# First gated rows two chunks later, the exponentials of two stages two chunks earlier, and the first gate load issued first

## The reference

```
scores = einsum('thpd,pnd->thpn', q, sub_keys)        # 8 heads, 2 x 128 keys
sv, si = top_k(scores, 16)
cand   = sv[:, :, 0, :, None] + sv[:, :, 1, None, :]
cv, ci = top_k(cand, 16)                              # 16 of 256 pairs per head
e_idx  = si0[ci // 16] * 128 + si1[ci % 16]
gates  = softmax(cv)
a      = einsum('thkd,td->thk', u_tab[e_idx], x)
wgt    = gelu(a) * gates
out    = einsum('thk,thkd->td', wgt, v_tab[e_idx])
```

## Time and profile before

| | |
|---|---|
| median of three executions | 1734.02 us |
| the profiled execution | 1737.73 us, its span 1735.8 us |
| TensorE busy | 1623.5 us, 94% of the span |
| VectorE busy | 1319.8 us, 76% |
| ScalarE busy | 689.5 us, 40% |
| GpSimd busy | 653.5 us, 38% |
| mean granted TensorE clock | 0.978 |
| chain that ended last | PE 70%, DVE 22%, DMA 4% |
| 8 stores of gates, issue to landing | 9.1 us shortest, 11.5 median, 28.3 longest |

### The profile page before, as it was taken

The page is one execution under the profiler, slowest core; times in us unless marked ns, Lnnn a source line. Parts: engine busy times, 40 slices in busy tenths (PEclk is TensorE's granted clock), DMA queues, the critical chain, the costliest instruction groups (busy, mean ns, idle before and its releaser), DMA issues.

```text
span 1735.8 us, 23134 instructions
## 1 busy us (share of the span) xinstructions
PE 1623.5 (94%) x8238; PEld 1376.8 (79%) x8238; DVE 1319.8 (76%) x2726; ACT 689.5 (40%) x1036; POOL 653.5 (38%) x450
## 2 busy tenths in 40 slices
PE   3999999986999999899986999999989999999996
PEld 3787776775899999899986898988966667766775
DVE  7489776987588899789934988988975555555589
ACT  4335565424333454545542343343323333333332
POOL 2010000002127788657652745746624423232311
PEclk9999999997999999999998999999999999999998
DMA  7423235453666567667767989889779999999962
GB/s 279 159 83 113 95 96 177 143 180 123 243 245 199 149 167 182 170 182 196 201 215 267 361 319 363 347 310 371 271 264 366 402 362 355 357 369 374 346 249 79
DMA packets 181682, 422.29 MB, mean 243 GB/s; under 512 B 33600, under 2 KB 66496, under 8 KB 181568
## 3 DMA queue, kind: packets, MB, share of 16 engines
q1 hardware_dynamic: 91472, 264.44, 42.5%
q0 software_dynamic: 57200, 139.58, 23.8%
q10 hardware_dynamic: 32896, 16.78, 3.5%
HBM read 375.55 MB, written 45.15 MB: 242 GB/s over the span
## 4 chain that ended last, share of the span: by engine, by line
PE 70%; DVE 22%; DMA 4%; ACT 2%; issue 2%; SPq 0%; DVEq 0%; ACTq 0%
PE bank L1676 21%; PE bank L1677 20%; PE bank L1678 20%; PE bank L1955 3%; DVE one L1468 2%; DVE one L1466 2%; DVE wlo L1300 2%; DVE one L1470 2%; DMA gates_by_key<-stage 2%; DVE raw L990 1%; DMA vraw<-in_v_tab_dram 1%; PE bank L1769 1%; PE bank L1754 1%; PE bank L1904 1%; DVE stats L1001 1%
## 5 line engine op out<-in xcount | busy, mean ns | idle before, releaser
L1676 PE MATMUL bank<-act_hi,whi 128*128 128x384 f32 (+1 forms) x1352 | 483.6, 358 | 22.4 <-ACT gelz L869 15.5
L1677 PE MATMUL bank<-act_lo,whi 128*128 128x384 f32 (+1 forms) x1352 | 473.9, 351 | 0.0
L1678 PE MATMUL bank<-act_hi,wlo 128*128 128x384 f32 (+1 forms) x1352 | 473.8, 350 | 0.0
L1676 PE MATMUL bank<-vhi,eh 128*128 128x512 f32 x768 | 305.4, 398 | 10.2 <-DVE vlo L1508 10.2
L1677 PE MATMUL bank<-vlo,eh 128*128 128x512 f32 x768 | 301.8, 393 | 0.0
L1678 PE MATMUL bank<-vhi,el 128*128 128x512 f32 x768 | 300.9, 392 | 0.0
L1676 PEld LDWEIGHTS bank<-act_hi,whi 128*128 128x128 f32 x1352 | 257.1, 190 | 40.5 <-issue 20.9
L1508 DVE TENSOR_TENSOR vlo<-vraw,vhi 128x512 fp32r<-128x512 f32 x256 | 176.6, 698 | 127.1 <-ACT vhi L922 126.4
L1677 PEld LDWEIGHTS bank<-act_lo,whi 128*128 128x128 f32 x1352 | 257.1, 190 | 14.0
L1678 PEld LDWEIGHTS bank<-act_hi,wlo 128*128 128x128 f32 x1352 | 256.2, 190 | 13.3
L643 POOL DMA_INDIRECT ring<-in_u_tab_dram,idxN x128 | 194.8, 1522 | 179.7 <-DVE ring L1305 138.7
(11 more groups left out here) (235 smaller groups left out, 1997.7 us busy)
## 6 DMA issues: line engine op xcount, KB each, us to landing
raw<-in_u_t_dram SPq DMA_DIRECT2D x128, 512.0 KB, 6.2
vraw<-in_v_tab_dram SPq DMA_DIRECT2D x256, 256.0 KB, 6.2
raw<-in_wblk_dram SPq DMA_DIRECT2D x61, 512.0 KB, 4.1
raw<-in_w_modt_dram SPq DMA_DIRECT2D x48, 512.0 KB, 4.0
gring<-gates_by_key SPq DMA_DIRECT2D x32, 768.0 KB, 9.0
gates_by_key<-stage ACTq DMA_DIRECT2D x8, 2048.0 KB, 11.5
gelu_ahead<-gelz SPq DMA_DIRECT2D x20, 768.0 KB, 4.2
gback<-gelu_ahead SPq DMA_DIRECT2D x40, 384.0 KB, 6.9
```

Of the source, the lines that this page charges most:

```text
L1676: mm(o, wh, mh, start=start, stop=False)
L1677: mm(o, wh, ml, start=False, stop=False)
L1678: return mm(o, wl, mh, start=False, stop=stop)
```

## The change

The exponential of stages 2 and 3 moves from step 24 of ScalarE's program to step 22. In FILL, the waits for the gates in ScalarE's and VectorE's programs move from step 4 to step 6, with the first rows behind them; rows that were made at steps 4 to 7 are now made at steps 6 and 7 and just after the loop, the first two chunks together. The number of operations is the same. In SyncE's program the load of chunk 88 of U is issued ahead of the waits, and the first load of gates ahead of the four rows of V.

```diff
-EXP_STEP = (11, 11, 24, 24)
+EXP_STEP = (11, 11, 22, 22)
...
+            load_u(PRE)
             for i in range(2):
                 sp.wait_ge(stage_out[i], 16 * (LAID * NBT // 16))
+            sp.wait_ge(gate_add, 16 * SLOTS)
+            load_g(0)
             for k in range(VR):
                 load_v(0, k, 0)
-            load_u(PRE)
-            sp.wait_ge(gate_add, 16 * SLOTS)
-            load_g(0)
             for c in range(PRE + 1, PRE + RAW):
                 load_u(c)
...
             for j in range(FILL):
                 ahead(SPILL + j)
-                if j == 4:
+                if j == FILL - 2:
                     for i in range(2):
                         act.wait_ge(stage_out[i], 16 * (LAID * NBT // 16))
-                if j >= 4:
-                    part_w(j - 4, j - 4)
-                if j >= 5:
-                    part_v(0, j - 5)
+                    part_w(0, 0)
+                    part_v(0, 0)
+                    part_w(1, 1)
+            part_v(0, 1)
+            part_w(2, 2)
+            part_v(0, 2)
             gelu(PRE - 1)
+            part_w(3, 3)
...
-                if j == 4:
+                if j == FILL - 2:
                     for i in range(2):
                         dve.wait_ge(stage_out[i], 16 * (LAID * NBT // 16))
                     dve.wait_ge(gate_add, 16 * SLOTS)
-                if j >= 4:
-                    weigh(0, j - 4)
-                    low_w(0, j - 4)
-                if j >= 5:
-                    low_v(0, j - 5)
-            for k in range(4, GR - 1):
+                    weigh(0, 0)
+                    weigh(0, 1)
+                    low_v(0, 0)
+                    low_w(0, 0)
+                    low_w(0, 1)
+            low_v(0, 1)
+            weigh(0, 2)
+            low_w(0, 2)
+            low_v(0, 2)
+            for k in range(3, GR - 1):
                 weigh(0, k)
                 low_w(0, k)
```

## The result

The changed kernel takes 1714.21 us, the median of four executions (1712.14 to 1714.45), against 1734.69 us for the kernel before, measured four times beside it (1733.91 to 1735.70). The ratio is 0.9879, with a 95% interval from 0.9862 to 0.9896: 1.2% faster, 20.5 us. The forecast was 1707 us in a range from 1700 to 1718. So the sign and the stated range held, and the forecast asked for 27.0 us where 20.5 came. The forecast's own range, 1701 to 1713 us, was missed: the time lies just inside the bracket of the first rival, 1713 to 1718. The profiled execution took 1714.44 us, its span is 1712.6 us, its mean granted clock 0.982.

The account below looks back on a forecast made before the run. TensorE is busy 94% of the span, so time is won only where it idles or clocks low. 7.9 + 8.6 + 10.4 = 26.9 us off 1737.73 gives 1710.8, less 3.7 is 1707; own range 1701 to 1713, stated 1700 to 1718.

Parts of the forecast that it names:

- the first rival: FILL: chunk 88 and four dots' gathers go ahead of the last store, 6.5 us; 1713 to 1718 us; chance 0.13.
- stage 2: TensorE's stall before the last one-hot piece goes, 5.43 us, with 2.5 of slow clock: 7.9 us.
- stage 3: TensorE's stall before the last one-hot piece goes, 5.74 us, with 2.9 of slow clock: 8.6 us.
- chunk 90's start in FILL: With the waits two steps later, TensorE starts chunk 90 at 946.9 rather than 958.27: 11.4 us earlier.
- clock behind chunk 90's stall: FILL: a stall longer than the earlier 2.95 us loses 2.5 us to slow clock against 1.6: -1.0 us.
- part 1: Stages 2 and 3: the exponential at step 22 removes both stalls and their slow clock, 7.9 and 8.6 us.
- part 2: FILL: waits two steps later; stalls of some 1, 3 and 5 us before chunks 88, 89 and 90; net 10.4 us.
- gates at 5.3 us: FILL: the first gate load lands 5.3 us after issue, at 922.8 against 927.8 before; upper bound 7.67 us.
- the two as equal: Last store: chunk 88 ahead costs 2.0 us, gathers starting 2.9 us later offset it; landing stays 28.33, 3 either way.
- The exponential wasn't it: Stages 2 and 3: another wait takes its place, gain half to nothing; 1715 to 1723.5 us; chance 0.08.
- more than summed: FILL: store's head start counts whole and chunk 89 isn't late, 3 + 2.3 us more; 1702 and below; chance 0.06.
- slower: FILL: ScalarE holds two gelus behind gates and V rows; decides if the store takes 55 us; chance 0.03.

Follow-up runs that it names:

- the first part alone: Kernel before with only the exponential of stages 2 and 3 moved from step 24 to 22: 1716.64 us, ratio 0.9898.
- Part 2: Changed kernel with the exponential back at step 24, leaving only the moved waits and SyncE's order: 1730.56 us, ratio 0.9976.

## Why the prediction came out as it did

The sum of the prediction and what the trace shows, term by term, in us of the span:

| term | predicted | measured |
|---|---|---|
| stage 2 | 7.9 | 8.06 |
| stage 3 | 8.6 | 8.62 |
| chunk 90's start in FILL | 11.4 | 7.50 |
| clock behind chunk 90's stall | -1.0 | -1.3 |
| rest of the way to the last stall, not foreseen | 0 | 1.7 |
| behind the last stall, not foreseen | 0 | -2.1 |
| shift before stage 2's end, not foreseen | 0 | 0.70 |
| span | 26.9 | 23.2 |

The rows behind chunk 90 are worked out from 24.88 us ahead at its start, 25.28 at the end of the last stall and 23.2 at the end; of the 1.7 us, 1.5 are the stall that is 1.92 us in one trace and 0.40 in the other. The last three rows come to 0.3 us together, so what is missing of the 26.9 us is the third row.

**Right: part 1.** Both stalls of the earlier trace rows went whole, with the slow clock behind them, and to 0.2 us by the sizes given. What the step took for granted, that the copies of gates and the gelu behind the exponential have cover, held: the first part alone gave even more than its 16.5 us. The drain behind a table load that the Trainium skill counts (ScalarE: Activation LUTs, What ACT_TABLE_LOAD costs) isn't there in the trace: the load is at 713.25 for 1.28 us, and the exponential starts at 714.54.

**Right in its mechanism, wrong in one size: part 2.** The mis-sized term is the landing of chunk 89 of U: "goes out near 919.8; with 8.5 us to landing". It took 13.86 us. The prediction had named its own sign for this, "VectorE waiting in FILL for chunk 89 much longer than 3 us", and the wait was 6.12 us. Of its three stalls, 1, 3 and 5 us, none came at its size: 2.25, 6.52 and 3.21. The load was issued 1.3 us sooner than worked out (901.15 is 21.5 us behind the point after stage 3, 919.8 was to be 22.7), so the copy ended 4.1 us late. From there on all steps were right: `low_u(89)` to `weigh(0, 2)` took 4.04 us, `weigh(0, 2)` to `weigh(0, 7)` 8.74 us (worked out: 8.9), and from there to chunk 90 4.49 us (4.49). These 4.1 us less the 0.2 are the 3.9 us missing in the third row. I had taken the 8.5 us from loads of the kernel before, and beside those no gather ran. This is the gathers' queue there from 918 to 927 us, of the kernel before:

```profile
q0 software_dynamic: 2, 0.00, 0.1%
```

In the changed kernel they run beside the load, since the dots of steps 5 and 6 came in front of VectorE's wait. The prediction saw these gathers, but charged them to the store, in rival 1, and not to the loads behind it. Holding the gathers back, and nothing else, brought the landing to 8.72 us and the time 7 us down, which shows the cause. Chunk 90 then starts 48.54 us behind the point after stage 3; the forecast had 946.9 - 897.07 = 49.8, the changed kernel has 53.70.

**Half right: gates at 5.3 us.** That is what they take where no gather is issued from number 8 on (5.36); in the changed kernel it is 7.1 us, within the bounds of 5.3 and 7.67 but above the 5 to 6 us that the prediction wanted to see. The store came 1.4 us sooner than 28.33, so the first `weigh` was 0.4 us late in all.

**Right: the store.** "I take the two as equal, with 3 us either way": 26.9 us. The two opposing terms show when each part runs alone. With part 1 alone the store is 28.33 - 25.85 = 2.5 us shorter (2.9 worked out), and GpSimd's first gather starts 5.0 us behind the store's issue (877.44 and 872.42), where it started 0.4 ahead of it (888.71 and 889.07): 5.4 us of late start rather than 2.9. That the late start is the cause fits, but no run moves it alone. Part 2 makes the store 30.73 - 28.33 = 2.4 us longer by itself and 26.9 - 25.85 = 1.1 us longer on top of part 1 (2.0 worked out). In the changed kernel that isn't the earlier dots' gathers: the store takes 26.9 us with gather 10 held too, and 28.29 us with gathers 8 and 9 or without. Chunk 88 in front is left, and with chunk 89 there as well it takes 1.0 to 1.4 us more. The equal counts of packets that this rests on are seen again, in a stretch where three queues are full:

```profile
q1 hardware_dynamic: 220, 0.77, 47.4%
q0 software_dynamic: 218, 0.77, 47.4%
q10 hardware_dynamic: 217, 0.11, 9.2%
```

The store's q10 moves as many packets as the two others but, with 512 bytes in each, a seventh of their bytes. By the rule of the Trainium skill (DMA: Bandwidth & Descriptors, Queues, rings and completion order) this is what going round packet by packet gives; the trace agrees.

**The rivals.** *The store is pushed out* didn't come true: 26.9 us, and 30.73 at most in any run. Its time, 1713 to 1718, is where the measurement lies, but for another cause: it asked for 6.5 us of store, and what came late was a load behind it. *The exponential wasn't it*, *more than summed* and *slower* are out: stalls gone, chunk 89 late, 1.2% faster.

**The base of the sum.** The sum went from the profiled execution, and I took 3.7 us off since the median lay so far below it. In the measurement beside the changed kernel, the profiled 1737.73 us lies 3.0 us above the median before and 1714.44 us lies 0.2 above that after. So the traces differ by 23.2 us where the medians differ by 20.5, and the sum took 3.7 us off besides. Half of the 7.2 us of error (1714.21 against 1707) comes from those 3.7 us: the sum without them is 1710.8. That the time still came within the stated range is luck in part, since the range reaches up to 1718 for a rival that didn't happen.

The other traces say where the excess lies. From chunk 90 to the last stall the kernels with the exponential moved alone, to step 22 and to step 23, run the program of the kernel before. They took 748.56 and 748.83 us there, the traced execution before 750.94; its stall of 1.92 us is 0.38 in both. So 2.1 to 2.4 us of it lie behind everything that the change touches, and taking them off was right for the kernel before. But the changed trace has 750.54 us there too, loses 2.1 us more behind the last stall, and yet lies only 0.2 us above its median. Why the changed kernel doesn't show the shorter time is open.

**What stays open.** Why the clock behind the last stall, the same 2.82 us in ten traces, is at full in some and at 0.66 in others; with one trace of each kernel it can't be told whether the kernel has a part in it. Nor was it tried whether the SyncE order of before would be as fast as the new one with the gathers held.

## What to carry over

When a wait moves back in a program, list what comes to stand ahead of it, and what that work lets others issue: here four dots cost VectorE nothing, but freed slots whose gathers took the transfer engines from the loads that the gated rows needed. Price a load's landing by what will run beside it in the changed kernel, not by the nearest row of the kernel before. And a producer that is needed at a known time should be taken from its place in the program by its own inputs: the exponential was ready 44 us early and cost 16.7 us for standing two steps too late, where one would have done.

## What the runs showed of the hardware

A load of 512 KB of U landed in 8.72 us or in 13.86 us, at the same place in SyncE's queue, with four gathers held back, or issued from 2.5 us before it to 3.7 us behind it. The 768 KB of gates took 5.36 us with no gather issued from number 8 on, and 6.92 us with gathers 8 and 9 issued 8.8 and 5.5 us ahead of them. A store of 2048 KB in packets of 512 bytes took 25.85 to 30.73 us in this place and 9.1 us at its shortest elsewhere; while three queues are full, its queue has a third of the packets and a tenth of the engines' time (217 of 655 packets in 4 us, 9.2%). What the granted clock takes behind a stall isn't set by its length alone: after 2.25 us nothing (1.00), after 6.52 us 0.76 over 6.4 us, after 3.21 us 0.58 over 6.8 us, and after the last stall of 2.82 us anything from 1.00 (six traces) to 0.65 over 8.8 us.
